# Where the shift of the first norm enters: before the first two blocks' products, or behind them as a bias

## The reference, cut to what matters

```python
mod = (silu(c) @ ada_w[0] + ada_b[0])          # 6144 values; the first 2048 are shift_m and scale_m
shift_m, scale_m, ... = split(mod, 6)
h = rmsnorm(x, norm_g[0, 0]) * (1 + scale_m) + shift_m
proj = h @ w_in                                # 1024 -> 3072: a_val, a_gate, q, k, v, g
a = a_val * sigmoid(a_gate)                    # then a convolution of 31 taps along the tokens
```

## Time and profile before

| | |
|---|---|
| median of 3 runs | 1183.22 us (1181.83 to 1185.23) |
| the profiled execution | 1181.65 us, span 1179.7 us |
| PE busy | 1124.4 us (95%) |
| VectorE busy | 811.4 us (69%) |
| ScalarE busy | 553.6 us (47%) |
| granted TensorE clock, mean | 0.983 of full |
| moved by the transfers | 246.43 MB, mean 209 GB/s |

### The profile page before, as it was taken

The page is one execution under the profiler, slowest core; times in us unless marked ns, Lnnn a source line. Parts: engine busy times, 40 slices in busy tenths (PEclk is TensorE's granted clock), DMA queues, the critical chain, the costliest instruction groups (busy, mean ns, idle before and its releaser), DMA issues.

```text
span 1179.7 us, 21770 instructions
## 1 busy us (share of the span) xinstructions
PE 1124.4 (95%) x9316; PEld 1003.0 (85%) x9316; DVE 811.4 (69%) x1382; ACT 553.6 (47%) x868; POOL 44.6 (4%) x71
## 2 busy tenths in 40 slices
PE   7899999999999998779999999999989999999898
PEld 4778678988878885469999999999978999988798
DVE  1598457888477875865666644578898956669855
ACT  3123525454110135463555533456677845468834
POOL 0010000000000000000000000000000000051000
PEclk8999999999999998999999999999999999999999
DMA  9877685899978853975455555534433354344242
GB/s 371 358 281 271 249 324 213 303 337 338 351 292 237 302 195 139 311 273 189 134 189 188 179 179 179 179 107 148 174 108 108 107 179 152 135 144 144 72 144 72
DMA packets 38288, 246.43 MB, mean 209 GB/s; under 512 B 4400, under 2 KB 5584, under 8 KB 9648
## 3 DMA queue, kind: packets, MB, share of 16 engines
q1 hardware_dynamic: 29072, 182.36, 44.7%
q0 software_dynamic: 6240, 43.94, 10.0%
q10 hardware_dynamic: 2880, 18.74, 3.8%
HBM read 225.24 MB, written 19.79 MB: 208 GB/s over the span
## 4 chain that ended last, share of the span: by engine, by line
PE 77%; DVE 11%; DMA 6%; ACT 4%; issue 2%; SPq 1%; ACTq 0%; DVEq 0%
PE ps L1429 15%; PE ps L1431 15%; PE ps L1433 15%; PE ps L1436 10%; PE ps L1532 4%; DMA ca_dram<-more 2%; DMA ring<-ca_dram 2%; PE ps L1505 1%; DVE ring_rounded L2193 1%; PE ps L1625 1%; DMA more<-in_ada_w 1%; PE ps L2047 1%; PE ps L1578 1%; DVE ada_more L2804 1%; PE ps L1516 1%
## 5 line engine op out<-in xcount | busy, mean ns | idle before, releaser
L1429 PE MATMUL ps<-sq_rounded,w_high_rounded 128*128 128x256 f32 x1136 | 327.5, 288 | 2.9 <-DVE ring_rounded L2193 1.6
L1433 PE MATMUL ps<-sq_rounded,ring_rounded 128*128 128x256 f32 x1136 | 322.5, 284 | 0.0
L2193 DVE TENSOR_TENSOR ring_rounded<-ring,w_high_rounded 128x1024 fp32r<-128x1024 f32 x214 | 253.6, 1226 | 90.0 <-ACT w_high_rounded L829 89.7
L1431 PE MATMUL ps<-hT_rounded,w_high_rounded 128*128 128x256 f32 x992 | 282.0, 284 | 0.0
L829 ACT ACTIVATE w_high_rounded<-ring 128x1024 fp32r<-128x1024 f32 x214 | 213.8, 1049 | 66.4 <-PE ps L1433 66.3
L1429 PEld LDWEIGHTS ps<-sq_rounded,w_high_rounded 128*128 128x128 f32 x1136 | 219.2, 193 | 10.6 <-issue 5.9
L1433 PEld LDWEIGHTS ps<-sq_rounded,ring_rounded 128*128 128x128 f32 x1136 | 219.2, 193 | 0.0
L1431 PEld LDWEIGHTS ps<-hT_rounded,w_high_rounded 128*128 128x128 f32 x992 | 191.7, 193 | 0.1
L1429 PE MATMUL ps<-more_rounded,w_high_rounded 128*128 128x256 f32 x448 | 128.0, 286 | 0.3 <-issue 0.3
L1433 PE MATMUL ps<-more_rounded,ring_rounded 128*128 128x256 f32 x448 | 127.3, 284 | 0.0
L1436 PE MATMUL ps<-big,ring 128*128 128x256 f32 x512 | 113.4, 380 | 0.0
(11 more groups left out here) (420 smaller groups left out, 1699.4 us busy)
## 6 DMA issues: line engine op xcount, KB each, us to landing
ring<-in_blocks SPq DMA_DIRECT2D x139, 1024.0 KB, 4.9
ada_w<-in_ada_w POOLq DMA_DIRECT2D x27, 1024.0 KB, 7.7
ada_more<-in_ada_w POOLq DMA_DIRECT2D x13, 1024.0 KB, 8.0
we_dram<-we_t ACTq DMA_DIRECT2D x8, 1024.0 KB, 9.0
ca_dram<-more ACTq DMA_DIRECT2D x8, 1024.0 KB, 12.1
ring<-we_dram SPq DMA_DIRECT2D x8, 1024.0 KB, 5.5
ring<-ca_dram SPq DMA_DIRECT2D x8, 1024.0 KB, 13.3
big<-in_ada_w SPq DMA_DIRECT2D x4, 1024.0 KB, 11.4
```

The source lines that it names most:

```text
L1429: nc.tensor.matmul(out, high[:, k, columns], x_high, start=start, stop=False, skip_group_check=True)
L1431: nc.tensor.matmul(out, high[:, k, columns], x_low, start=False, stop=False, skip_group_check=True)
L1433: last = nc.tensor.matmul(out, low[:, k, columns], x_high, start=False, stop=stop, skip_group_check=True)
L2193: nc.vector.tensor_tensor(rounded(w), w, w_high[:, c % 2, ks], ALU.subtract)\
```

## The change

The first two blocks multiply the normed tiles without the shift: `first_products` waits for VectorE's tile and no longer for ScalarE's shift. SyncE loads the scale pieces and the blocks' rows first; the four shift pieces follow, each behind a wait for the scale piece of the same number. TensorE makes the shift's rows behind all products of the two blocks (`shift_columns`), turns them once, and multiplies the two blocks' weights (still in `w_high_plain`) with the shift as one moving column (`shift_products`: 2 blocks, 2 halves, 8 tiles). The four resulting columns are copied to `shift_bias`; ScalarE adds them in the sigmoid, VectorE in the gated product, both now in two halves. The tiles get their shift on ScalarE behind the two blocks, for block 2 and those that follow. Rounding the tiles stands behind the first sigmoid, and VectorE's eight low parts stand behind the first 15 taps. A semaphore is saved by letting s5_dq count on `lam_here`.

```diff
@@ -277,6 +277,7 @@
         s5_dq = sb("s5_dq", [P, GROUPS // 4])
         we_t = sb_both("we_t", [P, 8, 2, P])
         last_weight, last_gain, eps_squared = s5_small[:, 19, 0:DT], s5_small[:, 19, DT:2 * DT], s5_small[:, 19, 2 * DT:2 * DT + 1]
+        shift_bias = s5_small[:, 19, 2 * DT + 4:2 * DT + 8]
         positions = s5_small[:, 0:4].rearrange("p a b -> p (a b)").bitcast(I32)
 
         we_dram = nc.dram_tensor("we_dram", (8, P, 8 * 2 * P), F32, kind="Internal").ap()
...
@@ -701,11 +702,14 @@
             sp.dma_start(const[:, 0:FIRST], dram["const"][:, 0:FIRST]).then_inc(const_here, 16)
             sp.dma_start(cols[:, :, :], dram["cols"]).then_inc(cols_here, 16)
             sp.dma_start(xT[:, :, :], dram["x"]).then_inc(x_here, 16)
-            def first_pieces(q):
-
-                for a in range(2):
-                    sp.dma_start((big, more)[a][:, 2048 * q:2048 * q + 2048], dram["ada_w"][QUARTERS * a + q])\
-                        .then_inc(ada0_here[q], 16)
+            def scale_piece(q):
+
+                sp.dma_start(more[:, 2048 * q:2048 * q + 2048], dram["ada_w"][QUARTERS + q]).then_inc(ada0_here[q], 16)
+
+            def shift_piece(q):
+
+                sp.wait_ge(ada0_here[q], 16)
+                sp.dma_start(big[:, 2048 * q:2048 * q + 2048], dram["ada_w"][q]).then_inc(ada0_here[q], 16)
 
             def first_weights(q):
 
@@ -713,16 +717,13 @@
                              dram["blocks"][0:TOGETHER, :, 2 * NB * q:2 * NB * q + 2 * NB].rearrange("b p x -> p b x"))\
                     .then_inc(w_here[q], 16)
 
-            first_pieces(0)
-            first_weights(0)
-            first_pieces(1)
-            first_weights(1)
-            sp.wait_ge(ada0_here[0], 32)
-            first_pieces(2)
-            first_weights(2)
-            sp.wait_ge(ada0_here[1], 32)
+            for q in range(3):
+                scale_piece(q)
+                first_weights(q)
             first_weights(3)
-            first_pieces(3)
+            scale_piece(3)
+            for q in range(QUARTERS):
+                shift_piece(q)
             def load_near(n):
 
                 sp.wait_ge(k_stored, 16 * (n + 1))
@@ -782,7 +783,7 @@
                 if n == PIECES + 4:
 
                     pool.dma_start(s5_small[:, 20:23], dram["s5_lam"]).then_inc(lam_here, 16)
-                    pool.dma_start(s5_dq[:, :], dram["s5_dq"]).then_inc(dq_here, 16)
+                    pool.dma_start(s5_dq[:, :], dram["s5_dq"]).then_inc(lam_here, 16)
                 if n == PIECES + 16:
                     pool.dma_start(s5_c[:, :, :, :], dram["s5_c"]).then_inc(c_here, 16)
 
@@ -824,6 +825,8 @@
                         act.wait_ge(blocks_done, first_block["s5_out"] + 2 + 2 * near_read)
                     else:
                         act.wait_ge(blocks_done, split_order[c - 2] + 1 if c >= 2 else TOGETHER)
+                        if c < 2:
+                            act.wait_ge(ada0_columns, QUARTERS + 2)
                     for half in range(2):
                         ks = slice(4 * half, 4 * half + 4)
                         nc.scalar.activation(w_high[:, c % 2, ks], ring[:, b % RING, ks], ACT.Copy)\
@@ -923,18 +926,27 @@
                 nc.scalar.activation(ada_rows[:, 0], FIRST_ROWS[q % 2][:, 0:NB], ACT.Copy).then_inc(ada0_copied, 1)
                 if q == 0:
                     norm_rstd(0)
-                tiles = range(2 * q, 2 * q + 2)
-                shift(0, 0, SHIFT_M, tiles)
-                for k in tiles:
-                    act.wait_ge(h_ready, k + 1)
-                    round_tiles(sq[:, k], hT[:, k])
+            act.wait_ge(ada0_parts, QUARTERS + 1)
+            act.wait_ge(ada0_columns, QUARTERS)
+            nc.scalar.activation(ada_rows[:, 0], SPARE[:, 0:NB], ACT.Copy).then_inc(ada0_copied, 1)
+            act.wait_ge(mods_ready, 1)
+            act.wait_ge(blocks_done, TOGETHER)
+            shift(0, 0, SHIFT_M)
 
 
             for j in range(2):
                 ps = unit("w_in", 2 * j)
                 if j:
                     act.wait_ge(a_ready, 1)
-                nc.scalar.activation(sgate, ps, ACT.Sigmoid).then_inc(sg_ready, 1)
+                    nc.scalar.activation(sgate, ps, ACT.Sigmoid).then_inc(sg_ready, 1)
+                else:
+                    act.wait_ge(shift_biased, 1)
+                    for i in range(2):
+                        ins = nc.scalar.activation(sgate[:, i], ps[:, i], ACT.Sigmoid, bias=shift_bias[:, i:i + 1], scale=1.0)
+                    ins.then_inc(sg_ready, 1)
+                    for k in range(DT):
+                        act.wait_ge(h_ready, k + 1)
+                        round_tiles(sq[:, k], hT[:, k])
                 for n in (*pieces_at("w_in", 2 * j), *pieces_at("w_in", 2 * j + 1)):
                     modulation_row(n)
             for j in range(4):
...
@@ -1604,11 +1616,29 @@
 
             def first_columns(q):
 
-                pe.wait_ge(ada0_here[q], 32)
-                for a in range(2):
-                    w = (big, more)[a][:, 2048 * q:2048 * q + 2048].rearrange("p (k n) -> p k n", k=KB)
-                    last = partial_rows(QUARTERS * a + q, w, FIRST_ROWS[q % 2], q, QUARTERS + q)
+                pe.wait_ge(ada0_here[q], 16)
+                w = more[:, 2048 * q:2048 * q + 2048].rearrange("p (k n) -> p k n", k=KB)
+                partial_rows(QUARTERS + q, w, FIRST_ROWS[q % 2], QUARTERS + q, QUARTERS + q).then_inc(ada0_parts, 1)
+
+            def shift_columns():
+
+                for q in range(QUARTERS):
+                    pe.wait_ge(ada0_here[q], 32)
+                    w = big[:, 2048 * q:2048 * q + 2048].rearrange("p (k n) -> p k n", k=KB)
+                    last = partial_rows(q, w, SPARE, 0, QUARTERS - 1)
                 last.then_inc(ada0_parts, 1)
+                first_turned(QUARTERS)
+
+            def shift_products():
+
+                pe.wait_ge(mods_ready, 1)
+                for b in range(TOGETHER):
+                    for i in range(2):
+                        at = 2 * PIECES * (QUARTERS + 1) + 2 * b + i
+                        for k in range(KB):
+                            last = nc.tensor.matmul(MISC[2][:, at:at + 1], w_high_plain[:, b, k, P * i:P * i + P],
+                                                    mod(0, SHIFT_M, k), start=(k == 0), stop=(k == KB - 1))
+                last.then_inc(ada0_columns, 1)
 
             def first_turned(q):
 
@@ -1620,7 +1650,7 @@
                 pe.wait_ge(w_here[q], 16)
                 ps, w = pair(bank_of(b)), w_high_plain[:, b]
                 for k in (2 * q, 2 * q + 1):
-                    pe.wait_ge(h_ready, k + 1)
+                    pe.wait_ge(hn_ready, k + 1)
                     for i in range(2):
                         last = nc.tensor.matmul(ps[:, i], w[:, k, P * i:P * i + P], hT[:, k], start=(k == 0 and i == 0),
                                                 stop=(k == KB - 1), skip_group_check=True)
@@ -1647,8 +1677,11 @@
             first_turned(3)
             for b in range(TOGETHER):
                 first_products(3, b)
+            shift_columns()
+            shift_products()
             for n in range(TOGETHER, 8):
-                project("w_in", n, (sq, mixT) if n in W_IN_SPLIT else (hT,))
+                project("w_in", n, (sq, mixT) if n in W_IN_SPLIT else (hT,),
+                        (lambda k: pe.wait_ge(h_ready, k + 1)) if n == TOGETHER else None)
                 for piece in pieces_at("w_in", n):
                     modulation(piece)
             pe.wait_ge(tables_here, 32)
@@ -2252,22 +2285,13 @@
                     ins = nc.vector.tensor_tensor(total, total, s[:, 4:6], ALU.add)
                 ins.then_inc(sq_sum, 1)
 
-            def by_quarter(x, q):
-
-                return x.rearrange("p (a q h) -> p q a h", a=2, q=QUARTERS)[:, q]
-
             sum_squares(0)
             for q in range(QUARTERS):
                 dve.wait_ge(ada0_columns, q + 1)
                 tiles = slice(2 * q, 2 * q + 2)
-                ins = nc.vector.tensor_tensor(by_quarter(mods[:, 0:2 * PIECES], q),
-                                              by_quarter(MISC[2][:, 2 * PIECES * q:2 * PIECES * (q + 1)], q),
-                                              by_quarter(col("ada_b")[:, 0:2 * PIECES], q), ALU.add)
-                if q == QUARTERS - 1:
-                    ins.then_inc(mods_ready, 1)
-                    dve.wait_ge(mods_ready, 1)
-                else:
-                    link(ins)
+                scales = slice(2 * PIECES * q + 2 * (QUARTERS + q), 2 * PIECES * q + 2 * (QUARTERS + q) + 2)
+                link(nc.vector.tensor_tensor(mod(0, SCALE_M)[:, tiles], MISC[2][:, scales],
+                                             col("ada_b")[:, DT + 2 * q:DT + 2 * q + 2], ALU.add))
                 link(nc.vector.scalar_tensor_tensor(out=gains[:, 0, tiles], in0=mod(0, SCALE_M)[:, tiles], scalar=1.0,
```

(34 more changed lines are left out.)

## The result

The changed kernel took 1193.76 us, median of 4 runs (1192.24 to 1195.58), beside 1183.49 for the kernel before on the same chip: a ratio of 1.0098 [1.0082, 1.0115], 10.3 us more by the medians, 11.6 by the ratio. The forecast was 1187.7, with a range up to 1191.3: right in direction, more than 2 us outside the range. The profiled execution took 1195.58 us (span 1193.8, mean clock 0.974; before 1181.65, 1179.7, 0.983), so its own difference of 13.9 us is larger than that of the medians; what the head adds has to be read from its marks, not from the whole.

A forecast was written before the change was run, and what follows sets the result against it. PE's own work was taken to bound the kernel, transfers deciding only at the head's start. Terms -9.3 + 3.8 + 1.1 + 7.2 + 1.7 = +4.5 us on 1183.2 gave 1187.7, range 1184.0 to 1191.3.

The forecast's parts named there:

- Steps 1 to 4: Head until the bias products: blocks' products end at 36.0, shift pieces take 3.8, chain to the column ends at 40.9.
- The gain of 9.3: Head's first part, through the two blocks' products: ends at 36.0 where before it was 45.3.
- Step 5: One-column bias products on PE: 64 records at 0.112 each, 7.2 us, ending at 48.1.
- step 7: Clock behind the one-column products: one stretch at the low clock, falling on block 2, costs 1.7 us.
- The rival with two low stretches: Two low-clock stretches, or one more in the head: 1.7 more, +6.2 in all, 1189.4; chance 0.20.
- Step 6: Tile shifts and the 1.28 table load lie under the one-column products; block 2 starts at 48.1, 2.8 later.
- just holds: At block 8, VectorE's halves are ready at 96.1 and 97.25, PE comes at 97.06: VectorE costs nothing.
- the first rival: Clock falls amid the one-column products, is up by block 2, costs nothing; VectorE sets +3.4, 1186.6; chance 0.20.
- The rival with unpaid loads: One-column products' weight loads cost nothing in place of 7.2; end 3.7 earlier, 1179.5; chance 0.06.
- three signs of being wrong: One-column products under 4.4 us, PE waiting for a shift piece, or delay at 60 us not that at the end.

The follow-up runs named there:

- the second experiment: Changed kernel with the shift column repeated to 128 moving columns on the same 64 weight loads: ratio 1.0048, median 1189.28 us.
- the second trace: The changed kernel profiled once more, with nothing altered: 1192.58 us.
- the first experiment: Changed kernel with only one of the eight products for each bias column: ratio 1.0036, median 1187.93 us.
- third: Changed kernel with bias operands swapped, the shift as 32-column weight and the blocks' weights streamed: ratio 1.0030, median 1185.91 us.
- fourth experiment: Changed kernel with the one-column products placed between those of block 2: ratio 1.0185, median 1206.32 us.
- the sixth: The third's kernel plus an early one-column sigmoid to load the table before the bias: ratio 1.0031, median 1185.63 us.
- fifth: The third's kernel plus VectorE shifting four tiles, low tiles before the taps, early sigmoid table, first shift piece before tile 6: ratio 1.0003, median 1183.35 us.

## Why the prediction was wrong in size

**Steps 1 to 4 held.** First piece worked on at 9.73 (forecast 9.5), products through at 36.21 (36.0), shift pieces 3.64 (3.8) with no wait for a transfer, bias products from 41.18 (40.9). The gain of 9.3 was 9.1.

**Step 5 failed**, and it is most of the miss: the term for the one-column products was mis-sized, 11.40 in place of 7.2, +4.2. The price of 0.112 was right for the full clock, as the first 20 records and the second experiment show. But step 7 of the same prediction said that the clock would fall behind such products, and step 5 was not worked out again for a fall within them. Some 23 records ran at 0.112, 41 at 0.213. The trace of the kernel before could have warned of it. Its records from 777.7 on, at a clock of 0.50, stream 256 columns, so their spacing says nothing of one column; but their loads of 128 columns took 0.33 us where the loads before them took 0.19:

```profile
778.20 0.33 PEld L1429 LDWEIGHTS ps<-sq_rounded,w_high_rounded 128*128 128x128 f32 x1
```

The Trainium skill, "TensorE: Matmul & The Clock Gate", section "LDWEIGHTS (loading the stationary operand)", gives the time of a load as its columns divided by 1.2 GHz, and makes no difference by the granted clock. As an estimate from it 64 loads are 6.8 us. The distance between records agrees with that at the full clock (0.112) and not at the low one (0.213); the measurement decides.

**Step 7 had the mechanism and was too small**: one stretch costing 1.7 on block 2 was forecast; the clock was low for 13.7 us, and blocks 2 and 3 lost 2.6, +0.9. With +0.3 from the start of step 5 that is 4.2 + 0.9 + 0.3 = 5.4, and 4.5 + 5.4 = 9.9, the measured delay of 9.86. The rival with two low stretches (+6.2) saw the right kind of thing, but it too priced the stretches on products with 256 columns alone.

**Step 6 was wrong, and the large step 5 hid it.** The table load does not lie under step 5; it waits for the bias. The first gated unit ended at 55.9: 4.5 of the 5.6 over the forecast are the later bias (52.6 for 48.1), the rest is the table load. That VectorE "just holds" came true because PE was late by nearly as much (9.9 and 11.1). The second experiment shows the error in the open. It is the first rival's case, no clock lost and VectorE setting the delay, for which the prediction had +3.4. The gated unit ended at 53.3, 3.1 behind the copied bias where the forecast had 1.9 (48.4 to 50.3); PE waited 1.6 at block 8, and the sum came 6.3 late. Its products had begun 1.7 later than forecast (42.58 for 40.9); without that it is 4.6, and the 1.2 over +3.4 is about the table load of 1.28 that the forecast had as hidden. In the cheaper versions VectorE set the delay, with waits of 3.4, 3.2, 2.8 and 1.3.

**The rival with unpaid loads** is refuted: 0.112 was paid for each even with one column, and more.

**None of its three signs of being wrong came**, and yet it was: the one-column products took over 4.4 us, PE waited for no shift piece, and the delay at 60 us (9.86) was that at 125 us (9.85) and nearly that of the medians (10.3). In the profiled execution itself it grew to 14.0 at the end, in the second trace it stayed at 11.0. The criteria had no upper price for step 5.

What stays open: why the runs of the first experiment have a median of +5.0 and both traces show +0 to 1 at the end. Neither is one of the slower runs, and unprofiled runs leave no rows.

## What to carry to other kernels

A price from a neighbouring row holds at the clock that row had. Where the added work may bring the clock down, price it at both levels, and take the low one for the work itself and not only for what follows. A product with one moving column still pays a full 128-column load for each tile: put the vector on the weight side with few columns and let the matrix stream (1.93 us in place of 11.40). And before PE is made faster, read which engine hands it its next block: here a bias for 1.93 us, with block 2 begun 1.9 sooner, still ended 3.5 late, since the way over ScalarE and VectorE to block 8 had grown (in the trace; 2.9 by the medians).

## What the runs showed of the hardware that was not expected

- The granted clock fell to 0.50 while PE had one-column products without a gap, in both traces of the changed kernel, and stayed at 1.00 with 128 columns on the same loads (one trace) and with the one-column products laid between those of 256 columns (one trace). More work for the array took less time (7.43 against 11.40 us).
- Weight loads of 128 columns took 192 ns at the full clock and 333 ns at the low one, and a record of one column came every 0.112 and every 0.213 us.
- A wait of 3.2 to 4.0 us of PE at block 8 was followed in the first, third and fourth experiment by a stretch at a clock of 0.54 to 0.89, one of 2.8 in the sixth by 0.62, so the wait was paid for again. Behind the waits of 1.6 and 1.3 in the second and fifth the clock stayed at 1.00.
- The table load of the sigmoid ran in front of its wait before the change and behind its wait after it, 1.28 us on the path. The code before has one wait ahead of the activation, the changed code two; that this is the reason was not tried.
